# Two-layer transformer on one core: the rounded weights move to three different residues modulo 512 bytes against the other matmul operands

## The reference

```
for layer in range(2):
    u = rmsnorm(h, mix_pre_g[layer])
    mixed = attention(u) @ w_out          # layer 0: latent + block, layer 1: stick-breaking
    h = h + rmsnorm(mixed, mix_post_g[layer])
    u = rmsnorm(h, ffn_pre_g[layer])
    gu = u @ ffn_w_gate_up[layer]
    f = (silu(gu[..., :2816]) * gu[..., 2816:]) @ ffn_w_down[layer]
    h = h + rmsnorm(f, ffn_post_g[layer])
```

## Time and profile before

| | |
|---|---|
| median of 3 runs | 1338.41 us (1338.32 to 1339.98) |
| span of the profiled execution | 1338.4 us |
| TensorE busy | 1297.8 us (97%), 6599 matmuls |
| weight loads busy | 1092.2 us (82%) |
| VectorE / ScalarE / GpSimd busy | 734.4 / 554.5 / 260.2 us |
| matmuls of `mm3` in the chain that ended last | 26%, 25%, 25% (lines 432, 434, 433) |

### The profile page before, as it was taken

How to read it: one execution, slowest core, us unless ns; L and a number is a source line. 1 busy time by engine, 2 the same in 40 slices (tenths; PEclk the granted TensorE clock), 3 DMA queues, 4 the chain that set the end, 5 groups by cost and what they waited for, 6 DMA issues and landing times.

```text
span 1338.4 us, 17696 instructions
## 1 busy us (share of the span) xinstructions
PE 1297.8 (97%) x6599; PEld 1092.2 (82%) x6599; DVE 734.4 (55%) x998; ACT 554.5 (41%) x885; POOL 260.2 (19%) x205
## 2 busy tenths in 40 slices
PE   6979999999999999999999999999999999999997
PEld 5667788898888888888898888887988888887885
DVE  4777655538645445422288788686575544553223
ACT  4466666546322332222364555464453222322112
POOL 0532200025211111000051111321431111110002
PEclk8999999999999999999999999999999999999999
DMA  4412222122333333333222111311223333332331
GB/s 158 128 49 64 72 72 71 48 79 80 110 97 101 101 94 92 89 98 94 84 75 68 48 48 55 87 48 48 80 86 104 94 94 98 100 115 79 95 95 63
DMA packets 190503, 112.34 MB, mean 84 GB/s; under 512 B 13696, under 2 KB 184773, under 8 KB 190446
## 3 DMA queue, kind: packets, MB, share of 16 engines
q1 hardware_dynamic: 188636, 106.81, 27.5%
q0 software_dynamic: 640, 2.10, 0.6%
q10 hardware_dynamic: 1170, 2.66, 0.5%
HBM read 109.43 MB, written 4.74 MB: 85 GB/s over the span
## 4 chain that ended last, share of the span: by engine, by line
PE 85%; DVE 8%; ACT 3%; issue 2%; POOL 1%; DMA 0%; POOLq 0%; ACTq 0%; SPq 0%; DVEq 0%
PE banks L432 26%; PE banks L434 25%; PE banks L433 25%; PE banks L1711 3%; DVE w_lo L427 1%; PE banks L1741 1%; PE banks L1629 1%; PE banks L1458 1%; DVE logits L1420 1%; PE banks L481 1%; DVE tf L701 1%; ACT logits L1431 1%; DVE probsT_lo L1470 1%; POOL stick_lo L1728 0%; DVE u_lo L711 0%
## 5 line engine op out<-in xcount | busy, mean ns | idle before, releaser
L427 DVE TENSOR_TENSOR w_lo<-w_raw,w_hi 128x1024 fp32r<-128x1024 f32 (+3 forms) x200 | 288.2, 1444 | 270.7 <-ACT w_hi L420 270.4
L432 PE MATMUL banks<-u_hi,w_hi 128*128 128x512 f32 (+1 forms) x1112 | 425.5, 383 | 5.8 <-DVE w_lo L427 4.3
L434 PE MATMUL banks<-u_hi,w_lo 128*128 128x512 f32 (+1 forms) x1112 | 419.5, 377 | 0.0
L433 PE MATMUL banks<-u_lo,w_hi 128*128 128x512 f32 (+1 forms) x1112 | 419.2, 377 | 0.0
L420 ACT ACTIVATE w_hi<-w_raw 128x1024 fp32r<-128x1024 f32 (+3 forms) x200 | 206.1, 1031 | 282.6 <-PE banks L434 282.5
L432 PEld LDWEIGHTS banks<-u_hi,w_hi 128*128 128x128 f32 x1112 | 210.6, 189 | 45.8 <-issue 4.9
L434 PEld LDWEIGHTS banks<-u_hi,w_lo 128*128 128x128 f32 x1112 | 210.3, 189 | 38.9
L433 PEld LDWEIGHTS banks<-u_lo,w_hi 128*128 128x128 f32 x1112 | 210.5, 189 | 38.0 <-issue 1.0
L904 POOL TENSOR_TENSOR up<-up,gate 128x512 f32<-128x512 f32 x44 | 71.9, 1635 | 375.1 <-DVE up L930 358.3
L885 ACT ACTIVATE gate<-gate 128x512 f32<-128x512 f32 x44 | 27.8, 632 | 202.2 <-DVE gate L926 202.2
L1728 POOL TENSOR_TENSOR stick_lo<-softplus,stick_hi 128x1280 fp32r<-128x1280 f32 x14 | 44.1, 3162 | 157.0 <-DVE stick_hi L1724 157.0
(11 more groups left out here) (256 smaller groups left out, 1983.1 us busy)
## 6 DMA issues: line engine op xcount, KB each, us to landing
w_raw<-in_ffn_w_gate_up_dram SPq DMA_DIRECT2D x88, 512.0 KB, 3.7
w_raw<-in_ffn_w_down_dram SPq DMA_DIRECT2D x30, 512.0 KB, 3.6
w_raw<-in_sb_w_qkv_dram SPq DMA_DIRECT2D x24, 512.0 KB, 3.8
w_raw<-in_ab_w_in_dram SPq DMA_DIRECT2D x17, 512.0 KB, 3.7
w_raw<-in_ffn_w_down_dram SPq DMA_DIRECT2D x16, 448.0 KB, 3.6
w_raw<-in_ab_w_out_dram SPq DMA_DIRECT2D x8, 512.0 KB, 3.9
w_raw<-in_sb_w_out_dram SPq DMA_DIRECT2D x8, 512.0 KB, 4.7
bias_by_distance<-bias_rows ACTq DMA_DIRECT2D x1, 2560.0 KB
```

What stands on the lines that cost most here:

```text
L427: dve.tensor_tensor(wl[:, c.slot, 0:w], raw[:, c.slot, 0:w], wh[:, c.slot, 0:w].bitcast(F32), ALU.subtract).then_inc(w_lo, 1)
L432: nc.tensor.matmul(o, lh, rh, start=start, stop=False, skip_group_check=True)
L433: nc.tensor.matmul(o, lh, rl, start=False, stop=False, skip_group_check=True)
L434: return nc.tensor.matmul(o, ll, rh, start=False, stop=stop, skip_group_check=True)
```

## The change

The rounded weights are no longer three equal slots one behind the other: `w_hi` and `w_lo` become single rows of 3200 numbers, in which the slots begin at 0, 1040 and 2112 numbers, that is 0, 4160 (8 x 512 + 64) and 8448 (16 x 512 + 256) bytes. A pad of 32 numbers (128 bytes) goes in front of the stage region and the reservation becomes 27392 numbers (214 x 512 bytes), so that the stage begins 128 bytes later and at the same residue as `u`. All users of the slots take them from a list of views; nothing else changes.

```diff
@@ -61,6 +61,7 @@
 NSLOT = 3
+SLOT_AT = (0, 1040, 2112)
 AHEAD = 2
@@ -208,6 +209,7 @@
+        sb(ctx, "stage_line_pad", [P, 32])
         with ExitStack() as at0:
@@ -266,7 +268,7 @@
-        sb(ctx, "stage_buffers", [P, 27680])
+        sb(ctx, "stage_buffers", [P, 27392])
@@ -275,8 +277,10 @@
         raw = sb(ctx, "w_raw", [P, NSLOT, 1024])
-        wh = sb(ctx, "w_hi", [P, NSLOT, 1024], F32R)
-        wl = sb(ctx, "w_lo", [P, NSLOT, 1024], F32R)
+        wh_all = sb(ctx, "w_hi", [P, 3200], F32R)
+        wl_all = sb(ctx, "w_lo", [P, 3200], F32R)
+        wh = [wh_all[:, at:at + 1024] for at in SLOT_AT]
+        wl = [wl_all[:, at:at + 1024] for at in SLOT_AT]
@@ -417,14 +421,14 @@
-            act.activation(wh[:, c.slot, 0:w], raw[:, c.slot, 0:w], ACT.Copy).then_inc(w_hi, 1)
+            act.activation(wh[c.slot][:, 0:w], raw[:, c.slot, 0:w], ACT.Copy).then_inc(w_hi, 1)
...
```

More of the change, by code:

```diff
@@ L426, in split_lo @@
             w = width(c.c0)
-            dve.tensor_tensor(wl[:, c.slot, 0:w], raw[:, c.slot, 0:w], wh[:, c.slot, 0:w].bitcast(F32),
+            dve.tensor_tensor(wl[c.slot][:, 0:w], raw[:, c.slot, 0:w], wh[c.slot][:, 0:w].bitcast(F32),
                               ALU.subtract).then_inc(w_lo, 1)
@@ L443, in project @@
                 s = slice(k * stride + at, k * stride + at + m)
-                last = mm3(o, wh[:, c.slot, s], wl[:, c.slot, s], xh[:, first + k, :], xl[:, first + k, :],
+                last = mm3(o, wh[c.slot][:, s], wl[c.slot][:, s], xh[:, first + k, :], xl[:, first + k, :],
                            start=(first + k == 0), stop=(first + k == total - 1))
@@ L571, in f_pe @@
                     xh, xl = operands(pe, at)
-                    last = mm3(bank(b), wh[:, c.slot, s], wl[:, c.slot, s], xh, xl,
+                    last = mm3(bank(b), wh[c.slot][:, s], wl[c.slot][:, s], xh, xl,
                                start=(at == 0), stop=(at == total - 1))
@@ L630, in out_part @@
                 s = slice(k * P, (k + 1) * P)
-                last = mm3(bank(OUT_BANKS[ch][n]), wh[:, c.slot, s], wl[:, c.slot, s], *o_at(k),
+                last = mm3(bank(OUT_BANKS[ch][n]), wh[c.slot][:, s], wl[c.slot][:, s], *o_at(k),
                            start=(k == 0), stop=(k == KD - 1))
@@ L640, in half_products @@
                 xh, xl = o_at(at + k)
-                mm = mm3(bank(b)[:, half(h)], wh[:, c.slot, s], wl[:, c.slot, s], xh[:, half(h)], xl[:, half(h)],
+                mm = mm3(bank(b)[:, half(h)], wh[c.slot][:, s], wl[c.slot][:, s], xh[:, half(h)], xl[:, half(h)],
                          start=(at + k == 0), stop=(at + k == total - 1))
@@ L784, in tile @@
                 s = slice(kk * P, (kk + 1) * P)
-                return mm3(bank(bs[n])[:, half(h)], wh[:, cs3[n].slot, s], wl[:, cs3[n].slot, s],
+                return mm3(bank(bs[n])[:, half(h)], wh[cs3[n].slot][:, s], wl[cs3[n].slot][:, s],
                            uh[:, kk, half(h)], ul[:, kk, half(h)],
@@ L824, in two_products @@
                 for cc, b in ((c, b0), (c.later(1), b1)):
-                    mm = mm3(bank(b), wh[:, cc.slot, s], wl[:, cc.slot, s], uh[:, k, :], ul[:, k, :],
+                    mm = mm3(bank(b), wh[cc.slot][:, s], wl[cc.slot][:, s], uh[:, k, :], ul[:, k, :],
                              start=(k == 0), stop=(k == KD - 1))
@@ L1066, in products @@
                 tok, cols = slice(t * P, (t + 1) * P), slice(half * T, (half + 1) * T)
-                return mm3(bank(b), hidh[:, k, tok], hidl[:, k, tok], wh[:, c.slot, cols], wl[:, c.slot, cols],
+                return mm3(bank(b), hidh[:, k, tok], hidl[:, k, tok], wh[c.slot][:, cols], wl[c.slot][:, cols],
                            start=(k == 0), stop=(k == KF - 1))
```

## The result

The changed kernel takes 1341.8 us (median of 16 runs, 1339.06 to 1343.82) against 1338.93 us for the kernel before (16 runs, 1338.24 to 1340.90). The ratio is 1.0019, with a 95% interval of 1.0012 to 1.0027: slower by 0.2%, where 1335.0 was forecast. The slot at 64 behaves as rival A said, at a smaller price.

What follows compares the result with a forecast made beforehand. TensorE, busy for 97% of the span, was taken as the bound. A saving of 6.1 us less 2.6 us for changes of offset gave -3.5 us on 1338.4, so 1335.0 us; range 1329 to 1346.

Steps and rivals of the forecast that it cites:

- rival A: Gate-up and projections: offset 64 behaves as 128 does, together +5.2 us, 1343.6 us; chance 0.33.
- Slot at 64: Matmuls with weights in that slot: taken as 226.6 ns, between bounds worth -2.2 and 9.3 us.
- Slot at 0: Matmuls with weights in that slot: settled distance 226.6 ns, as u has before the change.
- slot at 256: Matmuls with weights in that slot: 256 taken as equal to 0, from short query-weight stretches averaging 226.7 ns.
- Saving if every slot held 226.6: Hidden 3.1 us, last product 3.0 us, `so` and `oA` against `oB`, `cq` and `ckv` set off; sum 6.1 us.
- Changes of offset: Entering and leaving the slot at 64, some 66 turns with 2 changes: 20 ns each, 2.6 us lost.
- What else moves: 256-column matmuls, ScalarE and VectorE splitting, waits for `w_lo`: taken as 0, with some 1.5 us in the range.

Runs made afterwards that it cites:

- e4_slots_0_0_256: Changed kernel with its slots at 0, 0 and 256 bytes instead of 0, 64 and 256; 1332.7 us, ratio 0.9951 to the kernel before.
- e1_stage_only: Changed kernel with all three slots at 0, keeping the moved stage; 1333.71 us against 1340.40 for the kernel before, ratio 0.9949.
- e2_slots_only: Changed kernel with the stage back at its old residue, keeping the new slots; 1344.29 us, ratio 1.0030 to the kernel before.

## Why the prediction was wrong

The step that failed is "*Slot at 64.* ... I take 226.6". The chunks in that slot stand at 233.3 in gate, up and the down projection. The reason given there, that the `oB` stretches come to 226.6 from other starts, is about arriving at offset 0; it says nothing of a stream that stays at 64. The rows did not decide it either way: of the residues 0, 128, 256 and 384 two settle and two do not, which is an even split and not the exception that rival A makes of settling. The middle of the two bounds named, (225 + 233.4) / 2 = 229.2 ns, is the very value at which the prediction's sum changes its sign, so the rows supported no forecast of the sign. The forecast took the favourable side; at 233.3 rival A's side came about, which costs gate and up 5.0 us and keeps 1.1 of the 3.1 us from the down projection.

*Slot at 0* and *slot at 256* were right: 226.7 each (e4_slots_0_0_256).

*Saving if every slot held 226.6* was right in size: 3.1 and 3.0 us forecast, 3.07 and 2.90 measured where every slot does hold it (e1_stage_only). With two slots of three the down projection keeps 2.0 of its 3.1.

*Changes of offset* were counted as 132 of 20 ns. What is seen is one per turn, on entering the slot at 256 after that at 64: some 0.03 us in gate and up (7 distances of 231.4 for 226.6) and 0.05 in the last product (5.49 for 5.44); slot 0 comes settled behind it. The price of a change is above the 20 ns taken and their number is half, so the term, about 66 x 0.03 = 2.0 us by the first price, came near its 2.6 by two errors that offset each other.

*What else moves* was right: `w_lo` waits are 6.6 us in 6 as before, and VectorE and ScalarE are busy within 0.7 us.

*Rival A* had the place, but 5.2 us where the spans differ by 1.7 and the medians by 2.9. It took all 2880 matmuls of u to stand at 226.6. The 1968 of gate and up did, but the projections are broken into short streams that stood a little higher: 22 distances from 790.86 to 795.89 us had 228.8 ns before, and the same chunk has 233.4 after (790.74 to 795.87, slot at 64). Their third, 960 - 656 = 304 matmuls at 4.6 ns, is 1.4 us and not 1.9; begin and middle together grew by 0.6 only, where `so` and `oA` gain too (0.5 in the prediction's estimate); what more is absorbed between the streams was not taken apart. It priced 66 resettlings at 50 ns, 3.3 us, where 0.03 us each is seen in gate and up. Its gain of 4.1 us for the hidden stages was right (3.9), in the last product by a wrong way: the slot at 64 gained there too (229.6), since the operands change places and the offset becomes -64, and the slot at 256 gained less (228.8), since it settles again there.

The base was loose as well: the span of 1338.4 was set beside the median of 1338.41. The time of the profiled run after is 1.8 us above its span (1341.87 to 1340.1), and a run of the kernel before with a span of 1338.7 took 1340.51. By this estimate the profiled run of before was one of some 1340.2 us, above the median. Neither this nor rival A's price changes the sign.

The chances of 0.38 and 0.33 said that the choice was nearly even, and the range held the time; the sign was lost on one residue that no row showed.

## What to carry to other kernels

Where TensorE is the bound and loads weights for each matmul, read the distance between starts by buffer slot, not the busy time: TensorE was 97% busy with all slots at 0 and with all at 64 alike. As a thing to try, give streamed and loaded operands one residue modulo 256 bytes in every stage, which was worth 0.5% here, and remember that their difference changes sign where they change places. Where a value that no row shows decides the sign of a forecast, and its bounds lie on both sides, measure it first: one run with all slots at 64 would have shown it.

## What had not been expected of the hardware

The distance by offset is not symmetric: 64 has 233.3 ns; 192 has 229.5 in the down projection, and its like, -64, has 229.6 and 228.9 in the last product. The values repeat after 256 (0 and 256: 226.7; 128 and 384: 232.2 to 233.3 in e2_slots_only). Why 192 lies between is open, and so is why 16 and -16 have two values each. That the offset causes the gain and the loss is shown; by what part of the chip it does so is not.

226.67 and 233.33 ns, the two values that come most often, are 34 and 35 times 6.67 ns; whether the starts are held to such a grid, no run tested. The Trainium skill (TensorE: Matmul & The Clock Gate, "Back-to-back issue gap") gives 518 cycles for 512 columns as the gap of isolated matmuls, by estimate 215.8 ns at 2.4 GHz, and 131 ns per matmul for a sustained stream with weight loads; at none of the offsets tried does a stream come under 226.6, so no run here shows either.
